# Strassen's scheme for 16 of the 22 K-chunks of a down projection, on one core

## The reference, cut to what matters

```
def conv_glu_ffn(xn, w_up, conv_w, conv_b, w_down):     # xn: 512 x 1024
    h = xn @ w_up                                        # 512 x 5632
    hp = jnp.pad(h, ((0, 0), (2, 0), (0, 0)))
    hc = conv_b + sum(hp[:, j:j + s] * conv_w[j] for j in range(3))
    gate, up = jnp.split(hc, 2, axis=-1)
    return (jax.nn.silu(gate) * up) @ w_down             # 2816 = 22 * 128 rows
h = h + conv_glu_ffn(rmsnorm(h, norm2_g[l]), ...)
```

## Time and profile before

| | before |
|---|---|
| median of three runs | 1467.72 us (1467.67 to 1468.3) |
| profiled execution: span from first to last instruction | 1465.1 us |
| profiled execution's own device time | not given apart; the median is 2.6 us over the span |
| TensorE busy (matmul) | 1456.5 us, 99% |
| TensorE weight loads | 1205.3 us, 82% |
| DVE busy | 964.0 us, 66% |
| ACT busy | 671.7 us, 46% |
| GpSimd busy | 45.8 us, 3% |
| chain that ended last | 96% TensorE, 2% DVE, 1% ACT |
| DMA | 139.67 MB, 95 GB/s |

### The profile page before, as it was taken

The page is one execution under the profiler, slowest core; times in us unless marked ns, Lnnn a source line. Parts: engine busy times, 40 slices in busy tenths (PEclk is TensorE's granted clock), DMA queues, the critical chain, the costliest instruction groups (busy, mean ns, idle before and its releaser), DMA issues.

```text
span 1465.1 us, 19634 instructions
## 1 busy us (share of the span) xinstructions
PE 1456.5 (99%) x7055; PEld 1205.3 (82%) x7055; DVE 964.0 (66%) x1625; ACT 671.7 (46%) x1153; POOL 45.8 (3%) x34
## 2 busy tenths in 40 slices
PE   9999999999999999999999999999999999999998
PEld 7888888888888888888888888888888888888886
DVE  7877667655787734776477776665658776357753
ACT  8655555443544422343474555544344443234434
POOL 0000000002100000000200000000030000000001
PEclk9999999999999999999999999999999999999999
DMA  6322222232333233322432222222323322332331
GB/s 249 92 68 92 82 59 86 73 104 83 116 100 100 75 98 115 97 86 79 129 128 87 78 82 66 73 87 76 117 89 101 97 90 82 105 111 90 100 106 67
DMA packets 43673, 139.67 MB, mean 95 GB/s; under 512 B 5824, under 2 KB 5952, under 8 KB 43344
## 3 DMA queue, kind: packets, MB, share of 16 engines
q1 hardware_dynamic: 43024, 137.73, 29.8%
q10 hardware_dynamic: 576, 0.97, 0.2%
HBM read 136.52 MB, written 2.10 MB: 95 GB/s over the span
## 4 chain that ended last, share of the span: by engine, by line
PE 96%; DVE 2%; ACT 1%; issue 0%; DMA 0%; DVEq 0%; ACTq 0%
PE dense L655 28%; PE dense L656 28%; PE dense L657 28%; PE turned L738 2%; PE branch L765 1%; PE dense L925 1%; PE dense L927 1%; PE dense L926 1%; PE dense L670 1%; PE dense L672 1%; PE dense L671 1%; PE scores L730 1%; PE scores L727 1%; PE branch L751 1%; ACT tmp L1163 0%
## 5 line engine op out<-in xcount | busy, mean ns | idle before, releaser
L655 PE MATMUL dense<-hg,whi 128*128 128x512 f32 x1304 | 515.7, 395 | 0.2
L657 PE MATMUL dense<-hg,wlo 128*128 128x512 f32 x1304 | 508.3, 390 | 0.0
L656 PE MATMUL dense<-hg,whi 128*128 128x512 f32 x1304 | 507.9, 390 | 0.0
L1009 ACT ACTIVATE whi<-raw 128x1024 fp32r<-128x1024 f32 (+3 forms) x268 | 264.3, 986 | 435.1 <-PE dense L657 408.5
L1362 DVE TENSOR_TENSOR wlo<-raw,whi 128x1024 fp32r<-128x1024 f32 (+3 forms) x268 | 304.7, 1137 | 194.7 <-ACT whi L1009 192.9
L655 PEld LDWEIGHTS dense<-hg,whi 128*128 128x128 f32 x1304 | 245.4, 188 | 52.1 <-DVE wlo L1362 2.6
L657 PEld LDWEIGHTS dense<-hg,wlo 128*128 128x128 f32 x1304 | 244.8, 188 | 52.1
L656 PEld LDWEIGHTS dense<-hg,whi 128*128 128x128 f32 x1304 | 245.1, 188 | 48.2 <-issue 0.2
L655 PE MATMUL dense<-act,whi 128*128 128x512 f32 x528 | 207.2, 392 | 0.0
L657 PE MATMUL dense<-act,wlo 128*128 128x512 f32 x528 | 205.6, 389 | 0.0
L656 PE MATMUL dense<-act,whi 128*128 128x512 f32 x528 | 205.5, 389 | 0.0
(11 more groups left out here) (221 smaller groups left out, 1361.0 us busy)
## 6 DMA issues: line engine op xcount, KB each, us to landing
raw<-in_w_up SPq DMA_DIRECT2D x88, 512.0 KB, 3.5
raw<-in_w_gate SPq DMA_DIRECT2D x48, 512.0 KB, 3.5
raw<-in_w_in SPq DMA_DIRECT2D x26, 512.0 KB, 3.5
raw<-in_w_down SPq DMA_DIRECT2D x32, 384.0 KB, 3.0
raw<-in_w_out SPq DMA_DIRECT2D x16, 512.0 KB, 3.5
raw<-in_w_down SPq DMA_DIRECT2D x16, 320.0 KB, 2.9
raw<-in_w_down_last SPq DMA_DIRECT2D x10, 512.0 KB, 3.5
raw<-in_w_v SPq DMA_DIRECT2D x8, 512.0 KB, 3.5
```

Of the source, the lines that this page charges most:

```text
L655: mm(out, a, xhi, start=start, stop=False)
L656: mm(out, a, xlo, start=False, stop=False)
L657: return mm(out, b, xhi, start=False, stop=stop)
L1009: fn(whi[:, s, 0:cols], raw[:, r, 0:cols], ACT.Copy).then_inc(w_hi.sem, 1)
```

## The change

The 22 chunks are now 8 + 8 + 6 (`THIRDS`). The first 16 are two blocks of 8 chunks, and each block's contribution to the residual is computed by Strassen's scheme in Winograd's form. For one group g of four, the block of weights A has 2 x 2 quarters: rows are the output chunks 2g and 2g+1, columns the even and the odd chunks of the block (four of 128 each, Q = 512 columns of `raw`). The operand B has 2 x 2 quarters: even and odd chunks, and first and second half of the tokens (256 columns each, `H2`). Instead of eight quarter products there are seven, each of 4 chunks x 3 = 12 matmuls of 256 columns:

The core of the diff:

```diff
-HALVES = (12, 10)
+THIRDS = (8, 8, 6)
+NFAST = 2
+FAST = THIRDS[0]
+FP = FAST // 2
+FG = C // 2
...
+        s12, s34 = v_flat[:, 2 * S:2 * S + 2 * Q], q_flat[:, 6 * S:6 * S + 2 * Q]
+        fast_hi = {"a1": whi[:, 0, 0:2 * Q], "s34": whi[:, 1, 0:2 * Q], "s12": spare[:, 0:2 * Q], "a22": k_r[:, 4, 0:Q]}
+        PRODUCTS = {"p1": ("a1", 0, X_B11), "p2": ("a1", Q, X_B21), "p6": ("s12", Q, X_T2), "p5": ("s12", 0, X_T1),
+                    "p7": ("s34", 0, X_T3), "p3": ("s34", Q, X_B22), "p4": ("a22", 0, X_T4)}
...
+            def product(l, b, g, q_):
+                kind, at, op = PRODUCTS[q_]
+                w_hi_, w_lo_ = fast_hi[kind][:, at:at + Q], fast_lo[kind][:, at:at + Q]
+                pe.wait_ge(fast_l.sem, fast_l.at(l, at_split(b, g, kind)))
...
+                n = at_prod(b, g, q_)
+                if n >= 4:
+                    sig, e = frees(n - 4)
+                    pe.wait_ge(sig.sem, sig.at(l, e))
+                to = fast_bank(b, g, q_)
+                for i in range(FP):
+                    w = slice(i * P, (i + 1) * P)
+                    mm(to, w_hi_[:, w], x_op(i, 0, op), start=i == 0, stop=False)
+                    mm(to, w_hi_[:, w], x_op(i, 1, op), start=False, stop=False)
+                    last = mm(to, w_lo_[:, w], x_op(i, 0, op), start=False, stop=i == FP - 1)
+                last.then_inc(fast_p.sem, 1)
...
+                for b in range(NFAST):
+                    j = (b + 1) * FAST
+                    up_pair(l, j, 0)
+                    fast_down(l, b)
+                    up_pair(l, j + 1, 1, between=b)
...
+            def fast_down(l, b):
+                last = (b + 1) * FAST - 1
+                fast_split_lo(l, b, 0, "a1")
+                x_odd_lo(l, b, last, last // 2)
+                x_sums_lo(l, b, last // 2)
+                fast_split_lo(l, b, 0, "s12")
+                for g in range(FG):
+                    if g > 0:
+                        fold_in(l, b, g - 1, "p4")
+                    fold_in(l, b, g, "p1")
+                    fast_split_lo(l, b, g, "s34")
+                    fold_in(l, b, g, "p2")
+                    fast_split_lo(l, b, g, "a22")
+                    fold_in(l, b, g, "p6")
+                    if g + 1 < FG:
+                        fast_split_lo(l, b, g + 1, "a1")
+                    else:
+                        split_lo_ffn(l, 2 * (last + 2), 2, SLOT)
+                    fold_in(l, b, g, "p5")
+                    fold_u4(l, b, g)
+                    if g + 1 < FG:
+                        fast_split_lo(l, b, g + 1, "s12")
+                    fold_in(l, b, g, "p7")
+                    fold_u2(l, b, g)
+                    fold_in(l, b, g, "p3")
...
+            def x_sums(l, p):
+                own = 4 * p
+                pool.wait_ge(glu.sem, glu.at(l, 2 * p + 1))
+                if p > 0:
+                    pool.wait_ge(x_lo.sem, x_lo.at(l, p - 1))
...
+                nc.gpsimd.tensor_tensor(t1, b12, b11, ALU.subtract).then_inc(x_sum.sem, 1)
...
+            def sums_12(l, b, g):
+                e = b * FG + g
+                pool.wait_ge(pair_in[g % 2], pair_value(l, b, g))
+                if e > 0:
+                    before = at_split(b, g - 1, "s12") if g > 0 else at_split(b - 1, FG - 1, "s12")
+                    pool.wait_ge(fast_l.sem, fast_l.at(l, before))
+                nc.gpsimd.tensor_tensor(s12[:, 0:Q], raw_part(g, 2), raw_part(g, 3), ALU.add).then_inc(sum12.sem, 1)
+                pool.wait_ge(sum12.sem, sum12.at(l, 2 * e))
+                nc.gpsimd.tensor_tensor(s12[:, Q:2 * Q], s12[:, 0:Q], raw_part(g, 0), ALU.subtract).then_inc(sum12.sem, 1)
...
+                for b in range(NFAST):
+                    for p in range(b * FP, (b + 1) * FP - 1):
+                        x_sums(l, p)
+                    sums_12(l, b, 0)
+                    x_sums(l, (b + 1) * FP - 1)
+                    sums_34(l, b, 0)
+                    for g in range(1, FG):
+                        sums_12(l, b, g)
+                        sums_34(l, b, g)
```

More of the change, by code:

```diff
@@ L885, in up_pair @@
                     else:
-                        before = (h_mid if half else h_new, C - NBANK + 2 * j + i)
-                    up_unit(l, i, before, 2 * jj + i, first=lead and i == 0)
-            def down(l, half):
-                nk = HALVES[half] // 2
-                for u, m, part in down_order(half):
-                    f = DOWN0[half] + u
+                        before = (h_new, C - NBANK + 2 * j + i)
+                    up_unit(l, i, before, 2 * jj + i, first=isinstance(j, int) and j == 0 and i == 0)
@@ new lines, in _ @@
+                last = FF - 1
+                fn(stat[:, 1, 0:1], eps, ACT.Sqrt)
+                sum_hi(l, 1)
+                root(l, 1)
+                up_pair(l, 1, 1, 0, 0)
+                with act.Fori(1, FP) as it:
+                    up_pair(l, it * 2, 0, 0, it - 1)
+                    up_pair(l, it * 2 + 1, 1, 0, it, sums=it - 1)
+                for b in range(NFAST):
+                    j = (b + 1) * FAST
+                    up_pair(l, j, 0, b, j // 2 - 1)
+                    fast_down(l, b)
+                    up_pair(l, j + 1, 1, b + 1, j // 2, after=b)
+                    with act.Fori(j // 2 + 1, FF // 2 if b + 1 == NFAST else j // 2 + FP) as it:
+                        up_pair(l, it * 2, 0, b + 1, it - 1)
+                        up_pair(l, it * 2 + 1, 1, b + 1, it, sums=it - 1 if b + 1 < NFAST else None)
@@ new lines, in _ @@
+                if l == L - 1:
+                    down_last(l, last)
+                    continue
+                cols = NPLAIN // 2 * P
+                done = [None, None]
+                for u, m, part in down_order():
+                    f = DOWN0 + u
+                    split_hi_ffn(l, f, f % RAW, cols)
+                    if u == 0:
+                        conv_tap2(l, 0, 1, last)
+                    if u == 1:
+                        gated(l, NFAST, last, last // 2, 1)
+                    if done[0] is not None:
+                        norm_chunk(l, 1, done[0])
+                    done = [done[1], m if part == 1 else None]
@@ new lines, in _ @@
+                if l == L - 1:
+                    down_last(l, last)
+                    continue
+                done = None
+                for u, m, part in down_order():
+                    f = DOWN0 + u
+                    split_lo_ffn(l, f, f % RAW, NPLAIN // 2 * P)
+                    if u == 0:
+                        gated_lo(l, last - 1, 0)
+                        taps(l, 0, last, 1)
+                        hp_evac(l, 1, last, 1)
+                    if u == 1:
+                        gated(l, last, 1)
+                    if u == 2:
+                        gated_lo(l, last, 1)
+                    if done is not None:
+                        down_evac(l, u - 1, done)
+                    done = m if part == 1 else None
```

548 lines of the change are left out of this document (357 added, 191 removed).

## The result

The changed kernel takes **1485.7 us** (median of four runs, 1484.65 to 1485.93); the kernel before took 1467.7 us in the same comparison. The ratio is 1.012, with a 95% interval of 1.0106 to 1.0134.

A forecast was written before the change was run, and what follows sets the result against it. TensorE, busy 99% of the span at full clock, was taken as the bound. The terms -14.4 + 25.6 + 2.2 + 1.3 = +14.7 us, added to the 1467.7 us median, gave 1482.4 us, range 1463 to 1495.

The forecast's parts named there:

- TensorE, -14.4 us: Both layers' first 16 chunks: 768 wide matmuls at 0.227 us go, 1344 half-width at 0.119 come, saving 14.4 us.
- The 75%: Skill-page estimate that a half-width matmul costs some 75% of a full one, losing 56 us on TensorE; set aside for traced spacing.
- The shared door, +25.6: Groups of seven: GpSimd sums and DVE's two-SBUF-input instructions exclude each other; gaps cost 6.4 us per block, 25.6 over four.
- the step that laid one group out in order: Steady group, queues and waits laid out: DVE kept out about 3.1 us, waits 0.4; group takes 11.3 us, gap 1.3.
- Where the wait shows: In groups, p2 waits for its bank or a product for a low part; first group's p6 and p7 wait 2.5 us together.
- Rival (a): Groups: GpSimd's sums slip beneath the folds, TensorE stays the bound; 1456.8 us or up to 1464; chance 0.14 below 1464.8.
- Rival (d): Groups: a GpSimd wait on a low part closes a ring, moving groups past 12.2 us; 1505 us, chance 0.06.
- Layer 0 behind the last up pair, +2.2: Plain part of layer 0: units shrink but the chain behind the last up pair does not; 2.2 us more gap.
- rival (e): Groups of seven: short gaps let TensorE's clock fall to 1.2 GHz for part of the products; about 1510 us, chance 0.04.
- The begin of layer 1, +1.3: End of layer 0's plain part: DVE's split, evacuation and norm leave no slack before layer 1; 1.3 us, bounds 0 and 4.
- Up loops, 0: Up loops: column sums take 3.3 us per two pairs, under DVE's 5.3 idle; costed at nothing.
- transfers, 0: Weight loads: a group's 1024 KB takes 7.2 us, asked for about 18 us ahead; costed at nothing.

The follow-up runs named there:

- e1: Changed kernel with GpSimd's four weight sums per group covering only 8 of 512 columns, all waits and orders kept; 1460.7 us.
- e7: The kernel before, with 816 wide matmuls of three down projections each cut into two of 256 columns; 1478.4 us, ratio 1.0073.
- e3: Changed kernel with the four weight sums per group moved from GpSimd to DVE, column sums left on GpSimd; 1464.8 us, ratio 0.9982.
- e2: e1 plus four 512-column GpSimd additions per group that nobody waits for; 1466.2 us, ratio 0.9990.
- e9: Changed kernel with only each block's first group's weight sums on DVE, in e8's order; 1474.3 us, ratio 1.0047.
- e8: e3 with x_odd's low part before the second to fourth sums at block starts, and early splits behind layer 0's last up pair; 1461.1 us.
- e4: Changed kernel with ACT making the third unit's high part before waiting for the last gated product in layer 0; 1482.6 us, ratio 1.0099.
- e5: e3 with x_odd's low part before the second sum, the fourth sum behind s12's low part, and an early third-unit split on ACT and DVE; 1470.1 us.
- e6: e5 with the sums s1 and s2 back on GpSimd in every group; 1471.4 us, ratio 1.0025.

## Why the prediction was right, step by step

**TensorE, -14.4 us: nearly.** The spacing is 0.1200 us, not 0.119 (the groups of e1, and e7 by itself), so 1344 products cost 161.3 us and the term is -13.0. (The 75% that the prediction set against this is not "halfway", which would be 81%, but the place of 256 between 128 and 512 columns, as in e7; and it makes the loss some 55 us, not 56. No term hangs on it.)

**The shared door, +25.6: 25.9, with 1.1 of it spacing, so 24.8.** That the weight sums on GpSimd cause the loss, through DVE, is shown from four sides: without the sums' length the loss is gone (e1), with the sums on DVE most of it (e3), with idle sums on GpSimd DVE is stretched again (e2), and with the sums of one group moved, that group alone recovers (e9). The parts were a little off and made it up between them. A steady group takes 11.0 us instead of 11.3, so three lose 3.1 us instead of 3.9. The first group loses 3.0 us instead of 2.5 (p6 1.5, p7 1.1, the first product 0.35). With 0.3 for spacing that is the block's 6.4. I had DVE kept out for 3.1 us per group; it is 10.9 - 8.0 = 2.9 us in the steady groups and 3.1 by the whole execution. Its own work was 8.0 us, not 7.6, and the 0.4 us of waiting for its own results that I had added makes up for that. So the close total is in part luck. And the step that laid one group out in order, with every wait, is what made it right: the blocking alone, with sums that nobody waits for (e2), gives 6.4 us.

**Where the wait shows: nearly as stated.** In the steady groups only banks are waited for: p2 waits for its bank, 0.95 us in a block's second group and mostly 0.5 in the next two, and p6 in most groups another 0.3 for its own. Low parts are late in a block's first group alone, that of s1 and s2 for p6 (1.4 us), that of s3 and s4 for p7 (1.0). In the list of what the weight loads wait for, the 4.1 us are the four first groups' p7, and the 3.9, put down to `spare`, the p2 of the four second groups (0.96 at 486.09). The first row is TensorE's, at the p2 of the third group:

```profile
497.13 0.36 PE L1023 MATMUL branch<-act,whi 128*128 128x256 f32 x1 [0.33 <-DVE h L1932]
```

```profile
L1023 PEld LDWEIGHTS scores<-act,whi 128*128 128x128 f32 x128 | 24.4, 191 | 10.3 <-DVE wlo L1925 4.1 <-DVE spare L1925 3.9 <-issue 2.3
```

**Rival (a), the door harmless (0.14 for under 1464.8): wrong here.** e1's 1460.7 lies between its 1456.8 and 1464, but only because the sums' length is left out there.

**Rival (d), a ring of sum, high part, low part, next sum: wrong.** e1 keeps the ring whole and loses nothing.

**Layer 0 behind the last up pair, +2.2: 2.39** (2.28 and 0.11 us at two starts). But this gap had a second price that the term left out, the largest single part of what the forecast missed. In the windows of the changed kernel above, TensorE is busy for 0.50 of 2.60 us, then the granted clock falls to 0.83 and 0.51, its lower level of 1.2 GHz, for 3.1 us, and returns. Eight wide matmuls start 0.42 us after the one ahead instead of 0.227: **1.6 us**. I had priced a falling clock as rival (e), for the groups of seven, where it stayed at 1.00 throughout; it came behind one long gap instead.

**The begin of layer 1, +1.3: 2.0** (1.03 and 0.71 us ahead of two matmuls, and 0.1 behind each). DVE's splits and norm there have no slack, as said; the size was inside its bounds.

**Up loops, 0; transfers, 0: held.** No gap stands in the up loops of the changed trace. The load of 1024 KB landed faster than the row I used (7.2 us):

```profile
issues: line engine op xcount, KB each, median us to landing
...
raw<-in_w_fast SPq DMA_DIRECT2D x16, 1024.0 KB, 4.9
```

GpSimd's waits for this load (71 us in all, 3.8 us ahead of 485.89 above) are not the load's fault: GpSimd is simply done, and the slot comes free only with the group two before.

**Sum.** -13.0 + 24.8 + 2.4 + 1.6 + 2.0 = +17.8, and some 0.8 in gaps of under 0.4 us: +18.6 against 18.8 in the spans. Against my +14.7 the terms that were short are the clock (1.6), the spacing (1.4), layer 1's beginning (0.7), the gap in layer 0 (0.2) and the small gaps (0.8); the stalls of the groups were over-rated by 0.8. That is 3.9 us, for a miss of 4.1 in the spans. In the medians the miss is 3.3, because 1.8 us lie around the changed kernel's span and not the 2.6 that I had carried over: 0.8 us of luck. The step that failed is the plain start of layer 0: it priced the gap and not the clock behind it.

**What stays open.** That a group blocks DVE for 2.9 us when its sums are waited for and for 1.9 when they are not (e2) is measured. That this is because DVE's own instruction releases a sum into its next one is read from the timeline, where the meeting repeats every 11.0 us, and was not tried by itself. Nor was the lateness of the sums measured without their blocking.

## What to carry to other kernels

An idle engine is not a free one if it shares a port with a busy one: price a GpSimd instruction on SBUF data by what it takes from DVE's two-SBUF instructions, and compare that with what DVE would need to do the work itself (here 2.9 us against 2.0 per group). Look at what releases the instruction too: here the sum that DVE's own low part releases met DVE's next such instruction in every steady group. And where units get shorter, every chain that was hidden behind one of them has to be priced again, with the clock that a long gap can cost.

## What the runs showed of the hardware that was not expected

**A two-SBUF instruction of DVE is shut out for all of GpSimd's data phase, and one with a PSUM input for none.** Of two neighbours, the low part of 512 columns takes 1.67 us instead of 0.68, the fold from PSUM of 256 columns 0.41 as ever (490.28 and 491.87 above). It goes both ways: GpSimd's sum of 491.36 takes 1.75 us where its neighbour takes 1.29. The page SBUF — State Buffer of the Trainium skill (section 🔬 SBUF: two separate sides) says that the shared pair is an exclusive lock that the first to start holds for the whole instruction; the trace agrees in kind. The price was expected. That it would be cheaper to do the sums on the engine that was shut out was not.

**The same gap may or may not bring the clock down.** Behind the last up pair, TensorE is busy for 0.50 of 2.60 us in the changed kernel, and the clock is down less than a microsecond after the matmuls have resumed at 711.13. In e3 it is busy for 0.48 of 2.60, in the same place, with the same 2.28 us between, and the clock stays at 1.00 (e3's last three windows); so it does in e9. In e1 it falls. The runs' times say the same: e3's ten executions lie at 1464.42 to 1464.88 (six) and 1466.02 to 1466.41 (four), 1.5 us apart, which is the price of one such fall. Only the profiled executions show where the clock falls, but each has its mean granted clock: 0.998 to 0.999 in the six and 0.997, three times, to 0.998 in the four, where the fall in the windows above takes off 0.0012 (0.17 x 1.2 + 0.49 x 3.1 = 1.7 us of 1463). e1's one fast execution (1459.2, the other three 1460.6 to 1460.8) has 0.999 and the others 0.998. The scatter alone would prove little: of the kernels without such a long gap, e8, e4 and e5 scatter by 0.2 to 0.7 us, but e6, e7 and the kernel before by 1.1, 1.1 and 1.6. The page TensorE: Matmul & The Clock Gate of the Trainium skill (section What's actually happening) says that the number of matmuls at the lower clock at a kernel's start differs between runs of one kernel; here the same is seen of a fall in its middle.
